# A two-block transformer kernel: attention groups rebuilt in pairs of heads, with their steps spread into the next group

## What is computed

```python
def mixer_a(h, w_in, sinks, w_out, cos, sin):        # stage a
    q, k, v, z = split(h @ w_in)                     # 32 q heads of 64, 4 kv heads
    o = banded_attention(rope(q), rope(k), v, A_WINDOW, A_QBLOCK, sinks)
    return (o * jax.nn.silu(z)) @ w_out

def mixer_b(h, w_in, ..., w_out, cos, sin):          # stage b
    q, kc, vc, ks, vs, kw, vw, gates, z = split(h @ w_in)
    kcmp, vcmp = compress(kc, ...), compress(vc, ...)          # 15 blocks
    o_cmp, o_slc = nsa_cmp_slc(q, kcmp, vcmp, ks, vs)
    o_win = banded_attention(q, kw, vw, B_WINDOW, WIN_QBLOCK)
    g = jax.nn.sigmoid(gates)
    o = g[..., 0] * o_cmp + g[..., 1] * o_slc + g[..., 2] * o_win
    return (o * jax.nn.silu(z)) @ w_out
```

## Time and profile before

| | us |
|---|---|
| median of 3 runs | 2522.11 (2518.75 to 2529.11) |
| the profiled execution, its own time | 2520.6 |
| its span, first to last instruction | 2519.4 |
| TensorE busy | 2325.9 (92%) |
| DVE busy | 1556.2 (62%) |
| ACT busy | 1089.8 (43%) |
| window of stage a, its first z tile to its last output added | 333.3 |
| window of stage b, the same | 452.4 |

### The profile page before, as it was taken

How to read it: one execution, slowest core, us unless ns; L and a number is a source line. 1 busy time by engine, 2 the same in 40 slices (tenths; PEclk the granted TensorE clock), 3 DMA queues, 4 the chain that set the end, 5 groups by cost and what they waited for, 6 DMA issues and landing times.

```text
span 2519.4 us, 27562 instructions
## 1 busy us (share of the span) xinstructions
PE 2325.9 (92%) x10579; PEld 1844.6 (73%) x10579; DVE 1556.2 (62%) x2230; ACT 1089.8 (43%) x1610; POOL 297.6 (12%) x374
## 2 busy tenths in 40 slices
PE   5689999999899999999999989999998899889988
PEld 1268878777777888888888877777777667667666
DVE  7788768879785546556556554555544345555654
ACT  1054446533336434434435454444445234444433
POOL 6633211123221001001000000000000000000000
PEclk9899999999999999999999999999999899999999
DMA  9878846688776657657666544343464332232233
GB/s 336 320 240 290 273 157 215 208 262 284 247 261 208 224 192 233 209 195 240 197 210 211 179 161 144 119 133 119 137 201 142 121 101 84 84 101 84 84 105 129
DMA packets 225270, 468.54 MB, mean 186 GB/s; under 512 B 13850, under 2 KB 19188, under 8 KB 224500
## 3 DMA queue, kind: packets, MB, share of 16 engines
q1 hardware_dynamic: 196944, 388.78, 46.5%
q0 software_dynamic: 20480, 67.13, 8.2%
q10 hardware_dynamic: 7716, 10.88, 1.2%
HBM read 464.65 MB, written 2.10 MB: 185 GB/s over the span
## 4 chain that ended last, share of the span: by engine, by line
PE 80%; DVE 10%; ACT 4%; issue 3%; DMA 2%; POOL 0%; ACTq 0%; DVEq 0%; SPq 0%
PE banks L534 23%; PE banks L536 22%; PE banks L535 22%; PE banks L792 3%; PE banks L545 3%; DVE ada_acc_vec L1496 2%; ACT w_high L988 1%; DMA ada_w<-in_w_ada 1%; PE banks L801 1%; DVE ada_acc L1449 1%; DVE w_low L1428 1%; PE banks L883 1%; ACT scores L1292 1%; DVE scores L1825 1%; DMA raw<-in_w_ada 1%
## 5 line engine op out<-in xcount | busy, mean ns | idle before, releaser
L1428 DVE TENSOR_TENSOR w_low<-raw,w_high 128x1024 fp32r<-128x1024 f32 x674 | 822.5, 1225 | 693.5 <-ACT w_high L988 693.0
L988 ACT CAST w_high<-raw 128x1024 fp32r<-128x1024 f32 x674 | 700.4, 1045 | 784.5 <-PE banks L536 783.4
L534 PE MATMUL banks<-w_high,act_a_high 128*128 128x512 f32 (+1 forms) x1696 | 694.4, 409 | 14.3 <-DVE w_low L1428 8.4
L536 PE MATMUL banks<-w_high,act_a_low 128*128 128x512 f32 (+1 forms) x1696 | 669.0, 394 | 0.0
L535 PE MATMUL banks<-w_low,act_a_high 128*128 128x512 f32 (+1 forms) x1696 | 668.4, 394 | 0.0
L534 PEld LDWEIGHTS banks<-w_high,act_a_high 128*128 128x128 f32 x1696 | 327.1, 193 | 108.0 <-issue 37.9
L536 PEld LDWEIGHTS banks<-w_high,act_a_low 128*128 128x128 f32 x1696 | 325.9, 192 | 70.2
L535 PEld LDWEIGHTS banks<-w_low,act_a_high 128*128 128x128 f32 x1696 | 327.2, 193 | 61.3
L401 POOL DMA_DIRECT2D ada_w<-in_w_ada x256 | 187.2, 731 | 952.9 <-DVE ada_acc L1449 946.7
L534 PE MATMUL banks<-w_high,act_b_high 128*128 128x512 f32 x640 | 250.6, 392 | 0.8 <-DVE act_b_low L1653 0.8
L536 PE MATMUL banks<-w_high,act_b_low 128*128 128x512 f32 x640 | 249.6, 390 | 0.0
(11 more groups left out here) (335 smaller groups left out, 2299.6 us busy)
## 6 DMA issues: line engine op xcount, KB each, us to landing
raw<-in_w_ff SPq DMA_DIRECT2D x128, 1024.0 KB, 5.2
raw<-in_w_in SPq DMA_DIRECT2D x64, 1024.0 KB, 6.8
ada_w<-in_w_ada POOLq DMA_DIRECT2D x256, 256.0 KB, 5.1
raw<-in_b_w_in SPq DMA_DIRECT2D x44, 1024.0 KB, 5.0
raw<-in_a_w_in SPq DMA_DIRECT2D x36, 1024.0 KB, 5.1
raw<-in_w_ada SPq DMA_DIRECT2D x32, 1024.0 KB, 7.2
raw<-in_w_o SPq DMA_DIRECT2D x16, 1024.0 KB, 7.5
raw<-in_a_w_out SPq DMA_DIRECT2D x16, 1024.0 KB, 5.1
```

Source lines behind the costliest of these rows:

```text
L534: T.matmul(out, xh, wh, start=(k == 0), stop=False)
L536: last = T.matmul(out, xl, wh, start=False, stop=(k == c.nk - 1))
L988: A.copy(WH[:, h % SPL, :, :], split_ap(h)).then_inc(*done("high", h))
L1428: V.tensor_tensor(WL[:, h % SPL, :, :], split_ap(h), WH[:, h % SPL, :, :].bitcast(F32), ALU.subtract).then_inc(*done("low", h))
```

## The change

- Heads are taken in pairs (4 per group in stage a, 8 in stage b over both branches). pair_scores writes the two heads to banks 0 and 1, alternating between the row halves 0 to 63 and 64 to 127; pair_turn makes six transposes into banks 1 and 2; pair_values puts the outputs of four heads, both token blocks, into bank 3. DVE's mask, maxima and minus-maximum, and ACT's copy to `pt`, become one instruction for both heads (768 columns); exponentials stay one per head and block.
- All three parts of different pairs fall on the same steps: scores of pair i at 6 + 6i (stage a) or 7 + 3i (stage b), its transposes six steps later, its values with the next pair's transposes. Order in an interruption: transposes, values, scores. Groups overlap: the last pairs and the output transposes (step 37 in a, 40 in b, now banks 2 and 3) lie in the next group's steps.
- q_turn moves from step 1 to step 3; cmp_scores, cmp_turn, cmp_values from steps 2, 5, 7 to 5, 9, 11; cmp_turn uses bank 3 and not bank 0.
- Outputs are read in parts of four heads, one instruction for both token blocks. The factor 0.5 moves into the gate. In the sinks, the copy per group falls away.
- On ACT and DVE the attention part of a step now comes before the weight part.
- The first two output chunks are split into 12 "early" and 4 "late" tile steps; order: early 0, early 1, late 0, late 1, then chunks 2 and 3. Some SBUF addresses shift; the key buffer of stage b is now in the mask of stage a.

The diff, cut to its core (removed lines, which are those of the functions printed above, are left out):

```diff
+    def add_outputs(name, w):
+        for k0, nk, part in ((0, 12, "early"), (12, 4, "late")):
+            for n in range(2):
+                add((name, n, part), w, k0 * P, CH * n, nk, n, k0=k0, whole=KT)
+        for n in range(2, 4):
+            add((name, n), w, 0, CH * n, KT, n % 2)
...
+PAIRS = {"a": 4, "b": 8}
+FIRST = {"a": 6, "b": 7}
+GAP = {"a": 6, "b": 3}
+OO_STEP = {"a": 37, "b": 40}
+GROUP = 2 * KT
+
+
+def score_step(name, i):
+    return FIRST[name] + GAP[name] * i
+
+
+def turn_step(name, i):
+    return score_step(name, i) + 6
+
+
+def value_step(name, i):
+    return turn_step(name, i + 1) if i + 1 < PAIRS[name] else turn_step(name, i) + 3
+
+
+def stage_steps(chunks, name):
+
+    order = []
+    for g in range(GROUPS):
+        order.append(chunks[name + "_z", g])
+        if g + 1 < GROUPS:
+            order.append(chunks[name + "_q", g + 1])
+    for part in ("early", "late"):
+        order += [chunks[name + "_out", n, part] for n in range(2)]
+    order += [chunks[name + "_out", n] for n in range(2, 4)]
+    return [(c, k) for c in order for k in range(c.nk)]
...
+        def pair_scores(name, g, i, k_):
+            for b in (0, 1):
+                T.wait_ge(*emptied[b])
+            T.wait_ge(*of("kG_made", (name, g)))
             T.wait_ge(*of("qG_made", (name, g, 1)))
             for tt in range(NT):
                 c0, n = (0, P) if tt == 0 else (P, SEQ)
...
+                for e in range(2):
+                    o = e * HD
+                    mm = T.matmul(bank(e)[:, c0:c0 + n], qG[o:o + HD, i % 4, tt * P:(tt + 1) * P], k_[o:o + HD, 0:n],
+                                  start=True, stop=True)
+            mm.then_inc(*done("scored", (name, g, i)))
+            for b in (0, 1):
+                emptied[b] = of("scores_masked", (name, g, i))
+
+        def pair_turn(name, g, i):
+            for b in (1, 2):
+                T.wait_ge(*emptied[b])
+            T.wait_ge(*of("scores_exp", (name, g, i)))
+            for e in (1, 0):
+                for q in range(3):
+                    tr = T.transpose(bank(2 - e)[:, q * P:(q + 1) * P], sc[:, 2 * (i % 2) + e, q * P:(q + 1) * P], ident[:, :])
+            tr.then_inc(*done("weights_turned", (name, g, i)))
+            for b in (1, 2):
+                emptied[b] = of("pt_made", (name, g, i))
+
+        def pair_values(name, g, i, vals):
+            if i % 2 == 0:
+                T.wait_ge(*emptied[3])
+            T.wait_ge(*of("pt_made", (name, g, i)))
+            v0, v1 = (vals[:, tt, g * HD:(g + 1) * HD] for tt in range(2))
+            for e in range(2):
+                s, c0 = 2 * (i % 2) + 1 - e, (2 * (i % 2) + e) * HD
+                o0, o1 = bank(3)[:, c0:c0 + HD], bank(3)[:, SEQ + c0:SEQ + c0 + HD]
+                T.matmul(o0, pt[:, s, 0:P], v0, start=True, stop=True)
+                T.matmul(o1, pt[:, s, P:2 * P], v0, start=True, stop=False)
+                mm = T.matmul(o1, pt[:, s, 2 * P:3 * P], v1, start=False, stop=True)
+            mm.then_inc(*done("valued", (name, g, i)))
+            if i % 2 == 1:
+                emptied[3] = of("outputs_read", (name, g, i // 2))
...
+        def pair_hooks(name, g, rel, k_, vals):
+            for i in range(PAIRS[name]):
+                if rel == turn_step(name, i):
+                    pair_turn(name, g, i)
+            for i in range(PAIRS[name]):
+                if rel == value_step(name, i):
+                    pair_values(name, g, i, vals[i // 4])
+            for i in range(PAIRS[name]):
+                if rel == score_step(name, i):
+                    pair_scores(name, g, i, k_[i // 4])
+            if rel == OO_STEP[name]:
+                oo_turn(name, g)
+
+        def outputs_ready(name, c, k):
+            if k == 0 and c.name == (name + "_out", 0, "early"):
+                T.wait_ge(*of("turn_low", ("oo_" + name, GROUPS - 2, 1)))
+            if k == 0 and c.name == (name + "_out", 0, "late"):
+                T.wait_ge(*of("turn_low", ("oo_" + name, GROUPS - 1, 1)))
...
+            T.wait_ge(*emptied[3])
...
+        for s, (c, k) in enumerate(stage_steps(C, "b")):
+            for g in range(GROUPS):
+                rel = s - GROUP * g
+                if rel == 3:
                     q_turn("b", g)
...
+                if rel == 5:
                     cmp_scores(g)
...
+                if rel == 9:
                     cmp_turn(g)
...
+                if rel == 11:
                     cmp_values(g)
...
+                pair_hooks("b", g, rel, (keys["b"], kG2), (vs, vw))
+            outputs_ready("b", c, k)
+            mm_tile(c, k, STAT[c.name[0]])
...
+        def pair_exp(name, g, i):
+            A.wait_ge(*of("minus_max", (name, g, i)))
+            for e in range(2):
+                j, s = 2 * (i % 4) + e, 2 * (i % 2) + e
+                for tt in range(NT):
+                    c0, n = (0, P) if tt == 0 else (P, SEQ)
+                    A.activation(sc[:, s, c0:c0 + n], sc[:, s, c0:c0 + n], ACT.Exp, scale=R, bias=nm[:, i // 4, j, tt:tt + 1],
+                                 accum_out=sm[:, i // 4, j, tt:tt + 1]).then_inc(*done("scores_exp", (name, g, i)))
+
+        def before(name, g, i):
+
+            return (name, g, i - 2) if i >= 2 else (name, g - 1, PAIRS[name] - 2 + i)
+
+        def pair_store(name, g, i):
+            A.wait_ge(*of("weights_turned", (name, g, i)))
+            if g > 0 or i >= 2:
+                A.wait_ge(*of("valued", before(name, g, i)))
+            A.copy(pt[:, 2 * (i % 2):2 * (i % 2) + 2, :], banks[:, 5:7, 0:3 * P]).then_inc(*done("pt_made", (name, g, i)))
...
+        def pair_mask(name, g, i, mask):
+            br, j, s = i // 4, 2 * (i % 4), 2 * (i % 2)
+            both, top = sc[:, s:s + 2, :], mx[:, br, j:j + 2, :]
+            V.wait_ge(*of("scored", (name, g, i)))
+            if g > 0 or i >= 2:
+                V.wait_ge(*of("weights_turned", before(name, g, i)))
+            V.tensor_tensor(both, banks[:, 4:6, 0:3 * P], mask[:, :].unsqueeze(1).broadcast_to([P, 2, 3 * P]),
+                            ALU.add).then_inc(*done("scores_masked", (name, g, i)))
+            V.wait_ge(*of("scores_masked", (name, g, i)))
+            V.tensor_reduce(top[:, :, 0], both[:, :, 0:P], AX, ALU.max)
+            V.tensor_reduce(top[:, :, 1], both[:, :, P:3 * P], AX, ALU.max).then_inc(*done("row_maxed", (name, g, i)))
+            V.wait_ge(*of("row_maxed", (name, g, i)))
+            if name == "a":
+                sinks = nsk[:, GH * g + j:GH * g + j + 2].unsqueeze(2).broadcast_to([P, 2, NT])
+                V.scalar_tensor_tensor(out=nm[:, br, j:j + 2, :], in0=top, scalar=-R, in1=sinks, op0=ALU.mult,
+                                       op1=ALU.min).then_inc(*done("minus_max", (name, g, i)))
             else:
...
+                V.tensor_scalar(nm[:, br, j:j + 2, :], top, -R, None, ALU.mult).then_inc(*done("minus_max", (name, g, i)))
...
+        def add_outputs(g, u):
+            br, h0 = u // 2, 4 * (u % 2)
+            hs, g0 = slice(h0, h0 + 4), 32 * (br + 1) + GH * g + h0
+            V.wait_ge(*of("scores_exp", ("b", g, 2 * u + 1)))
+            V.reciprocal(rd[:, hs, :], sm[:, br, hs, :]).then_inc(*done("rd_step", ("b", g, u, 0)))
+            V.wait_ge(*of("rd_step", ("b", g, u, 0)))
+            V.tensor_tensor(gr[:, :, hs], rd[:, hs, :].rearrange("p h a -> p a h"), gts[:, :, g0:g0 + 4],
+                            ALU.mult).then_inc(*done("rd_step", ("b", g, u, 1)))
+            V.wait_ge(*of("rd_step", ("b", g, u, 1)))
+            V.wait_ge(*of("valued", ("b", g, 2 * u + 1)))
+            V.tensor_tensor(half_heads(ob), half_heads(bank(3)), gr[:, :, hs].unsqueeze(3).broadcast_to([P, NT, 4, HD]),
+                            ALU.mult).then_inc(*done("outputs_read", ("b", g, u)))
+            V.wait_ge(*of("outputs_read", ("b", g, u)))
+            o = oo[:, :, HD * h0:HD * (h0 + 4)]
+            V.tensor_tensor(o, o, ob.rearrange("p (a n) -> p a n", a=NT), ALU.add).then_inc(*done("branch_added", (g, u)))
+            V.wait_ge(*of("branch_added", (g, u)))
...
+        for s, (c, k) in enumerate(stage_steps(C, "b")):
+            for g in range(GROUPS):
+                rel = s - GROUP * g
+                for u in range(4):
+                    if rel == value_step("b", 2 * u + 1) + 1:
+                        add_outputs(g, u)
+                        if u == 3:
+                            oo_gate("b", g, of("branch_added", (g, 3)))
+                if rel == OO_STEP["b"]:
+                    turn_low("oo_b", g, DHI, DLO, 4 * g, 2)
+                if rel == 5:
                     cmp_weights(g)
...
+                if rel == 11:
+                    oo_begin(g)
+                for i in range(PAIRS["b"]):
+                    if rel == score_step("b", i):
+                        pair_mask("b", g, i, maskB)
+            rests(c, k)
```

(57 more changed lines are left out.)

401 lines of the change are left out of this document (114 added, 287 removed).

## The result

The changed kernel takes 2425.8 us (median of 4 runs, 2417.6 to 2433.4) where the kernel before takes 2524.3 (2518.8 to 2529.1): ratio 0.961, 95% interval 0.957 to 0.965. The forecast was 2426 us, with a range of 2405 to 2467. The profiled execution has an own time of 2433.4 and a span of 2431.8 us.

The account below looks back on a forecast made before the run. The prediction took TensorE, at nearly full clock, as the bound. Gains of 32.2 us in stage a and 63.5 in stage b took 2520.6 to 2424.9 us; the median lying 1.5 higher gave 2426, range 2405 to 2467.

Parts of the forecast that it names:

- The pair interruption: TensorE, both stages: transposes, values and scores of two heads take 3.0 us against 4.0 for two single heads.
- the lower end: Scores of a pair: the two row halves run side by side, 0.85 us, instead of one after the other, about 1.5.
- the first rival: Scores of a pair: halves don't overlap for wide operands, 31 to 41 us more, 2457 to 2467 us; chance 0.17.
- The wait at the bare transposes: Steps 12 (stage a) and 13 (stage b), no values: scores wait for ACT's copy, 1.1 and 1.05 us per group.
- Stage a: First rewritten stretch: tiles 239.9 us plus 61.2 for four groups, 301.1 us, a gain of 32.2.
- Stage b: Second rewritten stretch: tiles 239.9 us plus attention work, waits and clock falls, 388.9 us, a gain of 63.5.
- before the output transposes: Stage b, step 40, at three boundaries: output transposes stand 1.85 us behind DVE's cmp_weights, outputs, gate and low half.
- before cmp_turn: Stage b, step 41, at three boundaries: cmp_turn waits 2.5 us for bank 3, which the output transposes filled.
- half rate: Stage b boundaries: granted clock falls to half, 2.5 us counted once per boundary, 7.5 us in all.
- Margins of 0.1 us: Stage b, odd steps: with values in between, ACT's copy ends just in time, 0 to 0.15 us late.
- the second rival: Stage b: copy late by a cast at three odd steps per group, clock falls follow, 2440 to 2455 us; chance 0.17.
- The clock rival: Stage b: 3 us interruptions of transposes and narrow matmuls halve the clock grant, 211 us more, 2637 us; chance 0.04.

Follow-up runs that it names:

- the same-half experiment: Changed kernel with the odd heads' scores computed from the even heads' queries and keys, rows 0 to 63, same matmul counts: 2448.3 us, ratio 0.970.
- the yardstick: The changed kernel run again unaltered, as the measure for the runs beside it: 2420.5 us, ratio 0.960.
- the experiment with the bare scores later: Changed kernel with scores that share an interruption with transposes but no values moved one tile step later: 2407.4 us, ratio 0.955.
- three edits of a few lines each: Changed kernel with cmp_turn in bank 0, cmp_scores at step 4 and bare scores one step later, together: 2398.8 us, ratio 0.951.

## Why the prediction was right

- **The pair interruption.** Forecast 3.0 us, measured 3.0 (0.66, 1.38, 0.86, 0.10). The choice of the lower end, which rested on cmp_scores, held; had it been wrong, the first rival's 31 to 41 us more would have held, and the same-half experiment came 28 us above the yardstick. The prediction's citation of the Trainium skill, TensorEngine Tiling (Array Packing), Key Properties, agrees: tiles run in parallel.
- **The wait at the bare transposes.** Forecast 1.1 us in stage a and 1.05 in b, measured 1.1 in each (1.75 us from transposes to scores, 0.66 of it transposes).
- **Stage a.** Forecast 61.2 us beside the tiles' 239.9, measured 299.8 - 239.9 = 59.9. No wait at the output or q transposes, as forecast.
- **Stage b.** Forecast 149.0 beside the tiles, measured 143.3. By terms: before the output transposes 1.7 us from start to start for 1.85, before cmp_turn 2.1 for 2.5 (together 11.5 us for 13); bare transposes 4.4 for 4.6 with the small lateness; last group 1.7 for 1.9; half rate 1.4 for 7.5; the rest about 123 for 122. The one term that is clearly mis-sized is the clock: I charged 2.5 us per boundary by the stretch behind a 3.56 us standstill, and the standstills are now 1.6 and 2.0 us. 7 and 11 starts at half rate came in the two profiles, 0.2 us each. The row was the nearest in place, not in length, and it was one of several: behind the four standstills of 3.6 to 5.2 us in the kernel before came 8, 9, 2 and 2 half-rate tile starts, and behind its four of 2.2 us in stage a came none, 5, 8 and none.
- **One wait was missed**: values of step 34 wait for outputs (L857, 0.6 us in three times), 1.1 us from start to start in three groups.
- **Margins of 0.1 us** at odd steps of stage b held: the second rival (2440 to 2455) would have shown as waits before the scores of full interruptions, and the only 4 waits of scores are at the bare ones. With one cast more ahead of the copy they turn into 16, which is what that rival describes: 2455.8 us.
- **The clock rival** fell. Stage a was granted 1.00, stage b 0.99, with interruptions of 3 us and six transposes in a row. By the PE-mode transpose rule of the Trainium skill (TensorE: Matmul & The Clock Gate) the faster clock would not engage for transposes; no run here bears that out: they start 0.11 us apart, as the q transposes before, and the tiles around them 0.227. Their own time goes with the granted clock: eight took 1.97 us behind the 3.56 us standstill and eight q transposes 1.09 us, and the granted clock in the two stretches was 0.50 and 1.00. The rival's mechanism isn't empty, though: behind values and cmp_scores in one interruption, 3.3 us, the rate was halved for 6 to 8 starts at some boundaries (the experiment with the bare scores later), where it never was behind the 3.0 us of a full interruption in the changed kernel. That costs 1 to 2 us a time at most, not 211.
- **The sum.** The stages gave 102.3 us for 95.7, and 6.1 of the 6.6 us between them are the clock term; the medians differ by 98.5. The mechanism and its prices were right, but right to the microsecond is luck: repeated medians of this kernel were 2425.8 and 2420.5.

What stays open: why the part ahead of stage a varies by 14 us from execution to execution, and 7 us of the tiles' gain.

## What to carry to other kernels

Batching small work between big tiles paid three times here: in fewer changes of shape (not measured by themselves), in row halves that run side by side (29 us), and in cover for the other engine's copy (26 us). It paid in full only with that copy at the head of its queue (34 us), so choose the order on the helper engines anew for the batched form. When all work is packed, read what is left off the list of waits: three edits of a few lines each took out three of the five remaining waits here, for another 22 us. Price a clock fall by all standstills of about the same length, not by the nearest one in the code, and as a chance, since like standstills were followed by it in one group and not in the next.

## What the hardware showed

- Score matmuls of 64 rows with 128 and 256 moving columns overlap on the two row halves almost entirely (0.86 us for eight, four on each half; 0.85 for four alone; 1.50 for eight on one half), and the order in which they are issued doesn't matter, at least up to four in a row on one half.
- With a standstill of 0.94 us in each interruption stage a had no half-rate start. Behind 1.6 and 2.0 us close together the rate was halved for 4 and 3 starts at two of three boundaries of the changed kernel, and for 4 and 1 in its second profile; behind 2.0 us alone at none of three (cmp_scores one step earlier). Behind values and cmp_scores back to back, 3.3 us without any standstill, it was halved for 6 to 8 starts at 8 of 21 boundaries (seven profiles); with a tile between them, at none of six. What decides between the boundaries was not found.
- Transposes follow the granted clock too: eight took 1.09 us with the granted clock at 1.00 and 1.97 at 0.50.
- A copy or masked read of 768 columns from banks took 0.80 us on ACT and 0.96 on DVE, against 0.81 and 0.96 interpolated from other widths.
